# Two transformer blocks in one kernel: layers unrolled with one panel stream, and the banded heads' steps reordered

## The reference

```python
h = _rms_norm(x, in_norm_g[l]); y = h @ w_in[l] + b_in[l]
m_h = mlstm_chunkwise(...)         # 4 heads of 64, stabilised exponential gates
h_h = hgrn2_chunkwise(...)         # 4 heads of 64, decay per channel
s_out = swa_sink_attention(...)    # 8 query, 2 key heads of 64, window 128, RMS norm and rotation of q and k
x = x + concat([m_out, h_out, s_out]) @ w_out[l]
x = x + square(relu(_rms_norm(x) @ w_up[l])) @ w_down[l]
x = x + sigmoid(_rms_norm(x) @ w_ple_gate[l]) * _rms_norm(p[l] @ w_ple_proj[l])
```

## Time and profile before

| what | value |
|---|---|
| median of 3 runs | 3120.99 us (3120.82 to 3121.11) |
| profiled execution | 3119.96 us |
| its span, first to last instruction | 3118.2 us |
| PE busy | 2886.8 us, 93% of the span |
| DVE, ACT, POOL busy | 1637.1, 1113.8, 162.9 us |
| mean granted clock of PE | 0.947 |
| DMA | 281.06 MB, 90 GB/s |

### The profile page before, as it was taken

One profiled execution on the slowest core, in us unless ns is written; L12 is line 12 of the kernel. 1 busy time (PEld: TensorE's weight loads), 2 busy tenths in 40 slices (PEclk: granted clock), 3 DMA queues, 4 the chain that ended last, 5 costly groups with the idle time before them and its releaser, 6 DMA issues. The chain is left out here.

```text
span 3118.2 us, 37948 instructions
## 1 busy us (share of the span) xinstructions
PE 2886.8 (93%) x14756; PEld 2357.1 (76%) x14756; DVE 1637.1 (53%) x2921; ACT 1113.8 (36%) x1712; POOL 162.9 (5%) x160
## 2 busy tenths in 40 slices
PE   6988899999798899999987998899997998899998
PEld 5777788887686777888866877788886787778886
DVE  5736566655664557555665544553544543464442
ACT  6434322224353433222344344332322444332231
POOL 1200000002121000000020000000000000000000
PEclk9987899999898889999988999999998999999999
DMA  4110144443221013444403111222322210122322
GB/s 151 68 41 28 41 176 175 150 152 111 90 84 41 28 41 132 154 160 162 162 34 128 62 35 35 68 86 97 108 73 92 68 53 19 65 89 76 113 78 78
DMA packets 43282, 281.06 MB, mean 90 GB/s; under 512 B 6105, under 2 KB 6361, under 8 KB 11737
## 3 DMA queue, kind: packets, MB, share of 16 engines
q1 hardware_dynamic: 43096, 278.54, 25.7%
HBM read 276.42 MB, written 2.10 MB: 89 GB/s over the span
## 5 line engine op out<-in xcount | busy, mean ns | idle before, releaser
L304 DVE TENSOR_TENSOR low_panels<-raw_panels,high_panels 128x2048 fp32r<-128x2048 f32 (+3 forms) x218 | 469.3, 2153 | 325.9 <-ACT high_panels L292 325.8
L292 ACT ACTIVATE high_panels<-raw_panels 128x2048 fp32r<-128x2048 f32 (+3 forms) x218 | 392.5, 1801 | 475.3 <-PE bank L1492 152.0
L421 PE MATMUL bank<-mlp_h_high,high_panels 128*128 128x512 f32 x1152 | 457.1, 397 | 0.0
L421 PE MATMUL bank<-mlp_h_low,high_panels 128*128 128x512 f32 x1152 | 455.2, 395 | 0.0
L421 PE MATMUL bank<-mlp_h_high,low_panels 128*128 128x512 f32 x1152 | 455.0, 395 | 0.0
L421 PEld LDWEIGHTS bank<-mlp_h_high,low_panels 128*128 128x128 f32 x1152 | 215.9, 187 | 52.8
L421 PEld LDWEIGHTS bank<-mlp_h_high,high_panels 128*128 128x128 f32 x1152 | 216.0, 188 | 52.0
L421 PEld LDWEIGHTS bank<-mlp_h_low,high_panels 128*128 128x128 f32 x1152 | 216.0, 188 | 51.6
L446 PE MATMUL bank<-high_panels,h_high 128*128 128x256 f32 x704 | 213.1, 303 | 8.4 <-DVE arena L1179 7.8
L421 PE MATMUL bank<-h_high,high_panels 128*128 128x512 f32 x496 | 207.2, 418 | 0.2
L1492 PE MATMUL bank<-mlp_hid_high,high_panels 128*128 128x512 f32 x512 | 204.3, 399 | 0.0
(11 more groups left out here) (349 smaller groups left out, 5068.5 us busy)
## 6 DMA issues: line engine op xcount, KB each, us to landing
raw_panels<-in_w SPq DMA_DIRECT2D x238, 1024.0 KB, 4.9
raw_panels<-in_w SPq DMA_DIRECT2D x16, 384.0 KB, 3.2
raw_panels<-in_w SPq DMA_DIRECT2D x4, 960.0 KB, 4.7
raw_panels<-in_w SPq DMA_DIRECT2D x4, 768.0 KB, 4.3
row<-in_row SPq DMA_DIRECT2D x2, 1220.0 KB
x<-in_xT SPq DMA_DIRECT2D x2, 1024.0 KB, 6.1
raw_panels<-in_w SPq DMA_DIRECT2D x4, 512.0 KB, 3.5
mix<-in_rope SPq DMA_DIRECT2D x2, 1024.0 KB, 8.3
```

Source lines behind the costliest of these rows:

```text
L292: self.nc.scalar.activation(self.g.high[:, i % SPLIT, 0:raw.shape[1]], raw, ACT.Copy).then_inc(self.high_ready, 1)
L304: self.nc.vector.tensor_tensor(self.g.low[:, i % SPLIT, 0:w], raw, self.g.high[:, i % SPLIT, 0:w].bitcast(F32), ALU.subtract).then_inc(sel ...
L421: ins = nc.tensor.matmul(bank[:, :], w[a][:, k, c0:c0 + P], rhs[b][:, k0 + k, :], start=first and k == 0 and j == 0, stop=last and k == kt ...
```

## The change

The loops are gone: layers are Python loops, and every stage of every layer stands in the program. A `Stream` holds the panels of all four layers in order, and a `Panels` view of one layer counts from its offsets, so that the two panels ahead may belong to the next layer. Each stage makes its own semaphores; Pool clears those of the stage before. The gains, biases and vectors of all layers are loaded once at the start, the mask `causal` goes to the second part's table, which is loaded in `layer_two`, and 1 + scale times gain is made in `embedding_gate`.

```diff
+class Stages:
+    def begin(self):
+        self.old = self.now
+        stack = ExitStack()
+        self.now = (Semaphores(self.nc, stack, self.n), stack)
+        self.n += 1
+        return self.now[0], [] if self.old is None else list(self.old[0].made.values())
+def clear(pool, used):
+    for sem in used:
+        pool.sem_clear(sem)
-def clear_semaphores(nc, s):
...
+class Stream:
+    def __init__(self, nc, g, s, layers):
+        ...
+        for dram, l, panels in layers:
+            for panel, (at, w) in zip(panels, offsets(panels)[0]):
+                if panel[0] != "w_mod_2":
+                    self.split.append(len(self.all))
+                self.all.append((dram[l, :, at:at + w], w))
...
 # Panels (a view of one layer; n0, i0 are its offsets in the stream)
+    def loads(self, sp, first, last):
+        lo = RAW + (0 if self.i0 == 0 and first == AHEAD else self.stream.upto(self.i0 + first))
+        for n in range(lo, min(self.stream.upto(self.i0 + last) + RAW, len(self.stream.all))):
             sp.wait_ge(self.low_ready, n - RAW + 1)
+            self.stream.load(sp, n)
     def high(self, act, i, products=None, value=0):
+        j = self.i0 + i
+        if j >= len(self.stream.split):
             return
...
 # part_one, start block
-                pan.load_first(sp, 0, s("first_panel_loaded"))
+                for n in range(RAW):
+                    views[0].stream.load(sp, n)
+                # (biases, vec2 and the final gain of all layers, then a wait for them)
+                for i in range(AHEAD):
+                    views[0].low(dve, i)      # ACT: views[0].high(act, i), behind its exponentials
-        with nc.Fori(0, DEPTH) as l:
-            layer_one(...)
+        for l in range(DEPTH):
+            layer_one(nc, g, a, views[l], l, k1, vecs[:, l, :], row, gbs[:, l, :], cs, bounds[:, l, :, :], small)
+            mlp_one(nc, g, views[l], l, vecs[:, l, :])
+            embedding_gate(nc, g, a, views[l], l, vecs[:, l, :], vec2[:, l, :])
...
 # layer_one
+                clear(pool, used)                       # Pool, behind its memset
-                norm_scalar(nc, act, g, e, hh, before={0: lambda: pan.high(act, 0), 3: lambda: pan.high(act, 1)})
+                norm_scalar(nc, act, g, e, hh)
-                norm_vector(..., before={1: lambda: pan.low(dve, 0), 4: lambda: pan.low(dve, 1)})
+                norm_vector(nc, dve, g, e, x, vec[:, V_GIN:V_GIN + DC], hh, hl)
 # DVE, token groups: the low split now follows the eviction
-                    if i == at_panel[n]:
+                    if i == at_panel[n] and kind != "token":
                         pan.low(dve, n + AHEAD)
...
+                        if i == at_panel[n]:
+                            pan.low(dve, n + AHEAD)
 # PE, levels
-                    if k == 15:
+                    if k == 18:
                         turn_gates()
-                    if k == 17:
-                        spread(0)
+                spread(0)                               # behind the last step
 # ACT: conv_open, sigmoid and exponential of step 17 now behind keep_apart(n_levels - 1)
 # DVE: gates(4) of step 16 now behind keep(n_levels - 1)
-            dense_m.setdefault(3 * i // 4, []).append(j)
+            dense_m.setdefault(i // 2, []).append(j)
 # DVE, blocks: the groups' evictions now ahead of block_probs(j)
-                    if 10 <= j < 14:
-                        rotate(j - 10)
+                    if j == 8:
+                        invert_window()                 # reciprocal of ss, then w_rstd; roots on ACT at j == 7, was 9
+                pool.wait_ge(s("w_rstd"), 1)            # Pool, behind the spans
+                for t in range(NT):
+                    rotate(t)                           # the same operations, on nc.gpsimd
 # banded heads
-        masked = region(7168, 1536, "p (i t) -> p i t", i=3)
+        masked = region(7168, 1536, "p (i t) -> p i t", i=6)
+        def score_bank(p, m):
+            return bank[3 + 2 * (p % 2) + m]
+        def chunk_bank(c):
+            return bank[1 + (chunk_after[c] + 1) % 2]
-                    if p >= 1:
-                        pe.wait_ge(w.max_ready, 2 * p)
+                    if p >= 2:
+                        pe.wait_ge(w.max_ready, 2 * (p - 1))
-                        nc.scalar.activation(turned[:, m, 0:n], bank[5 + m][:, 0:n], ACT.Copy)...   # twice
+                    nc.scalar.activation(turned[:, :, 0:n], bank[7]...[:, :, 0:n], ACT.Copy).then_inc(w.turned_kept, 1)
+                    behind = [chunk_at[c] for c in chunk_after if chunk_after[c] == i - 1]
+                    if behind:
+                        pe.wait_ge(chunk_low, max(behind) + 1)     # a group waits for the chunk in its bank
 # PE, step p (ACT: softmax(p), keep_turned(p - 2), then silu, groups, chunks; DVE: softmax(p), normalise(p - 3), ...)
-                    if 2 <= p < n_pairs + 2:
-                        result(p - 2)
-                    if 1 <= p < n_pairs + 1:
-                        turn(p - 1)
-                    chunks, then dense groups
+                    if 3 <= p < n_pairs + 3:
+                        result(p - 3)
+                    if 2 <= p < n_pairs + 2:
+                        turn(p - 2)
+                    dense groups, then chunks
...
 # embedding_gate (ACT high and DVE low alike), and mlp_two through its last calls
-                    if c == 2:
-                        pan.high(act, first + 4, full, DC + 2)
+                    if c in (2, 4, 6):
+                        pan.high(act, first + 3 + c // 2, full, DC + c)
-                pan.load_next_layers(sp, l)
```

More of the change, by code:

```diff
@@ L252, in __init__ @@
             self.first.setdefault(panels[n][0], i)
-        self.nsplit = len(self.split)
-    def loads(self, sp, l, first, last):
-        lo = RAW if first == 0 else self.upto(first) + RAW
-        for n in range(lo, min(self.upto(last) + RAW, self.n)):
-            sp.wait_ge(self.low_ready, n - RAW + 1)
-            self.load(sp, l, n)
     def upto(self, i):
         return 0 if i <= 0 else self.split[min(i, self.nsplit) - 1] + 1
-    def load(self, sp, l, n):
-        a, w = self.off[n]
-        sp.dma_start(self.g.raw[:, n % RAW, 0:w], self.dram[l, :, a:a + w]).then_inc(self.loaded[n % RAW], 16)
@@ L297, in low @@
+        if j >= len(self.stream.split):
             return
-        for n in range(self.upto(i), self.split[i]):
-            between(dve, n)
-        n = self.split[i]
-        w = self.off[n][1]
-        dve.wait_ge(self.high_ready, i + 1)
+        n = self.stream.split[j]
+        for m in range(self.stream.upto(j), n):
+            between(dve, m - self.n0)
+        w = self.stream.all[n][1]
+        dve.wait_ge(self.high_ready, j + 1)
         raw = self.g.raw[:, n % RAW, 0:w]
-        self.nc.vector.tensor_tensor(self.g.low[:, i % SPLIT, 0:w], raw, self.g.high[:, i % SPLIT, 0:w].bitcast(F32),
+        self.nc.vector.tensor_tensor(self.g.low[:, j % SPLIT, 0:w], raw, self.g.high[:, j % SPLIT, 0:w].bitcast(F32),
@@ L305, in low @@
                                      ALU.subtract).then_inc(self.low_ready, 1)
     def parts(self, pe, i):
-        n = self.split[i]
+        j = self.i0 + i
+        n = self.stream.split[j]
         pe.wait_ge(self.low_ready, n + 1)
-        kt, w = self.panels[n][2], self.off[n][1]
-        return [t[:, i % SPLIT, 0:w].rearrange("p (k c) -> p k c", k=kt) for t in (self.g.high, self.g.low)]
+        kt, w = self.panels[self.split[i]][2], self.stream.all[n][1]
+        return [t[:, j % SPLIT, 0:w].rearrange("p (k c) -> p k c", k=kt) for t in (self.g.high, self.g.low)]
@@ L1576, in _, with embedding_gate @@
                 nc.vector.tensor_tensor(g.mod_all[:, l, :], g.bank[7][:, 0:6 * DC], vec[:, V_BMOD:V_BMOD + 6 * DC], ALU.add)
-def embedding_gate(nc, g, a, s, pan, l, vec):
+    g.stages.end()
+def embedding_gate(nc, g, a, pan, l, vec, vec2):
+    s, used = g.stages.begin()
     x = g.x
@@ L2205, in _, with mlp_two @@
                     dense(i)
-    mlp_two(nc, g, s, pan, l, vec, mod)
-    clear_semaphores(nc, s)
-def mlp_two(nc, g, s, pan, l, vec, mod):
+    g.stages.end()
+def mlp_two(nc, g, pan, l, vec, mod):
+    s, used = g.stages.begin()
     x = g.x
```

400 lines of the change are left out of this document (193 added, 207 removed).

## The result

The changed kernel takes 3009.43 us (median of 4 runs, 3004.78 to 3011.59) against 3120.9 us for the kernel before (3117.34 to 3121.11). The ratio is 0.9644, with a 95% interval of 0.9632 to 0.9655. The profiled execution took 3004.78 us.

What follows compares the result with a forecast made beforehand. PE's own work, its holes and its slow-clock stretches were taken as the bound, with only holes and slow stretches winnable; terms summed to -77.4 us on a 3118.2 us span, giving 3043.5 us, range 3012 to 3080.

Steps and rivals of the forecast that it cites:

- three boundaries: Layer boundaries: clearing, barrier, jump back and per-layer loads go, leaving 6.49 us each; -36.9 us.
- end of the program: Program end: one clearing and loop exit go, idle before the last spreading falls from 3.97 to 2.09 us; -1.9 us.
- start, to the first product: Program start: the first two panels' splits now precede the norm with nothing hiding them; +2.6 us, bounds 0 and 5.
- levels, to the first block's scores, two layers: Gated heads' levels: two queue-order waits go and the clock recovers; -10.5 us a layer, bounds -14 and -6.
- blocks and rotation, to the first pair's scores: Block stage: window projections packed into 6 blocks, rotation moved to Pool; -3.3 us a layer, bounds -10 and +18.
- banded heads, to the end of the layer: Banded heads: second score banks, single copy and longer lag cut idle and slow clock; -8 us a layer, bounds -21 and +2.
- splits at the tails, and the rest: Three stage tails: splitting the next layer's panels delays DVE's last x updates, 0.8 us a place; +2.4 us.
- the clock holds: Rival, chance 0.14: PE stays at the upper clock level through levels and banded heads; 3013 us.
- code-loading rival: Rival, chance 0.03: each of 12 unrolled stage starts pays for its first instructions; at 8 us each, 3140 us.
- the eviction ahead of the split: Levels: evicting a token group before the low split was to help by 2 us.
- Pool's rotation: Block stage: Pool instead of DVE rotates the banded heads, taking 23 us a layer, with PE waiting for it.
- the rival that rested on this: Rival, chance 0.09: Pool's reads are locked out, the rotation takes 43.5 + 3 instead of 23 us; 3090 us.

Runs made afterwards that it cites:

- after_h32: The changed kernel with 8 unused columns (32 bytes) ahead of the stage tensors, no instruction changed: 3047.37 us, 0.9779 of the kernel before.
- rotate_dve: The changed kernel with the window heads' rotation back on DVE, four pieces at blocks 10 to 13: 3005.9 us, 0.9631 of the kernel before.
- lag_two: The changed kernel with the banded heads' old lag (transposes one pair behind, results two), new banks and buffers kept: 3005.14 us, 0.9632 of the kernel before.
- buffers_old: The changed kernel with the banded heads' old lag, one pair of score banks, three score buffers and one eviction per head: 3027.16 us, 0.9701 of the kernel before.

## Why the prediction missed

At equal pitch the forecast can be read term by term. The run after_h32 has the pitch of the kernel before (233.3 ns in all four feed-forward stages) and otherwise the whole change; its span is 3043.3 us, where the forecast's span was 3040.8.

| term | predicted, us | before to after_h32, us |
|---|---|---|
| three boundaries | -36.9 | -36.6 (2.08 + 4.39, 2.08 + 4.55 twice, as in the changed kernel) |
| end of the program | -1.9 | -1.9 (the same) |
| start, to the first product | +2.6 | +3.4 |
| levels, to the first block's scores, two layers | -21.0 | -19.9 |
| blocks and rotation, to the first pair's scores | -6.6 | -14.3 |
| banded heads, to the end of the layer | -16.0 | -7.4 |
| splits at the tails, and the rest | +2.4 | +1.8 (the remainder) |
| sum, on the span | -77.4 | -74.9 |
| pitch of the products | 0 | -40.4 (after_h32 to after: 3043.3 to 3002.9; by the medians -37.9) |

**The step that failed** is in the first paragraph: "The change leaves the matmuls as they are, so it can win only holes and slow stretches." It leaves their number and order, not their duration. The diff showed that tables in front of the activations changed their sizes and places; I read it for what it loads and not for where it puts the rest. The forecast of 3043.5 us is the time of the changed kernel with the old pitch (3047.37) within 4 us. None of the rivals was the right one: "the clock holds" gives 3013 us, near the result, but by another mechanism; the clock rose from 0.947 to 0.958 already in the part that was forecast (0.960 in after_h32).

**Boundaries, end, levels.** Right in place, mechanism and size. No stage start shows the hole of the code-loading rival: 2.08 us of idle ahead of the spreading at all three boundaries. In the levels DVE is late next, by up to 2.9 us, as forecast. Inside the levels one term was too small: the eviction ahead of the split was put at 2 us a layer, and undoing it cost 6 (83.6 to 89.9 us). Undoing the order cost 11. Together that is more than the 10 us a layer that the levels gained at equal pitch, so the two overlap.

**Start.** Right in sign, 0.8 us too small.

**Blocks and rotation.** The gain was forecast 8 us too small, and the reason I gave was wrong. Pool's rotation itself came out as forecast: 21.0 us from 208.02 to 229.05 (23 predicted), as these rows of Pool in the first layer show, its first operations and its last:

```profile
208.02 1.26 POOL L740 TENSOR_TENSOR arena<-arena,small 128x640 f32<-128x640 f32 x1 [60.41 <-DVE small L1352]
209.35 1.54 POOL L741 TENSOR_TENSOR arena<-arena,row 128x640 f32<-128x640 f32 x1
210.97 2.15 POOL L747 TENSOR_TENSOR arena<-arena,cos_sin 128x80 f32<-128x80 f32 x4
...
228.70 0.35 POOL L750 TENSOR_TENSOR arena<-arena 128x80 f32<-128x80 f32 x1
```

But it bought nothing: DVE can do it at no cost that was measured. What paid is a line that I had counted only in the levels ("evicting a token group before the low split helps by 2 us there"): over the levels and the blocks it is worth 15 us by the medians.

The rotation did meet one large operation of DVE with both inputs in on-chip memory, the squares of the heads' outputs:

```profile
209.94 2.04 DVE L1357 TENSOR_TENSOR arena<-arena 128x1024 f32<-128x1024 f32 x1
```

It began while Pool's second operation ran and took 2.04 us, where rotate_dve and the kernel before have 1.22 us for it. Pool's next operation, the first of the four at 210.97, began while it ran and took 1.22 us, where the median of its kind is 0.35. In both cases the one that came second was the one drawn out. By the Trainium skill, "SBUF — State Buffer", section "Who interferes with whom", Pool's reads are locked out while DVE holds two SBUF inputs, and the other way round. The trace agrees, at 0.8 us for DVE and 0.9 for Pool in this layer. Pool's operations of 640 elements stayed at 1.26 and 1.54 us, far from the 23.5 us a layer of the rival that rested on this.

**Banded heads.** Half the size that was forecast, and won by the second pair of banks, the six buffers and the single eviction (22 us between lag_two and buffers_old), not by the lag. I had listed all of them and priced none by itself. Undoing them costs more than the whole stage had gained on the kernel before (90.3 us in buffers_old, 86.4 before). Either the rest of the change in this stage (the chunks on the projections' banks, among others) cost something, or buffers_old is worse than the old arrangement because both heads share bank 7; that was not separated.

## What to carry to other kernels

Before costing a change, compare not only the instructions but also where its tensors will lie: a table that changes its size moves everything allocated behind it, and here 32 bytes were worth 34 to 38 us of 3000, as much as the three boundaries together. When a kernel is tuned, try a few pads ahead of the operands of its dense stages, and when two versions are compared, hold the distance between those operands equal. And of a set of edits made together, the cheapest (one eviction ahead of one split, 15 us) can be the one that pays while the most elaborate ones (rotation on Pool, longer lag) pay nothing.

## What the runs showed of the hardware

The pitch of back-to-back products of 128x128 by 512 columns, in stages with a mean granted clock of 0.97 to 0.99, depended on the distance between the stationary and the moving operand in on-chip memory: 226.7 to 229.2 ns at 0, 64, 256, 512 and 832 bytes modulo 1024, 232.3 or 232.4 at 128 and 233.3 or 233.4 at 32, 96 and 800, with one stage at 832 that ran at 233.3 where its twin ran at 228.9. A common shift of both operands by 32 bytes made no difference. Why the distance matters, no run shows. By the Trainium skill, "TensorE: Matmul & The Clock Gate", section "Step-by-step: what each phase is for", the two operands are read through two independent ports; by "SBUF — State Buffer", section "Who interferes with whom", TensorE never waits on anyone. Neither has a place for what these runs show, and here the measurement decides.

The granted clock of a layer differed between kernels with the same instructions. The second run of `layer_one` of the changed kernel, and then that of after_all32, which is the same code with everything shifted (columns as above):

```profile
800.00:1124.20 324.20, 294.13 (x1912) 246.62 (x1912) 183.49 (x411) 148.98 (x294) 55.74 (x74) 0.91 0.16 54
```
```profile
801.00:1130.30 329.30, 299.84 (x1913) 251.59 (x1913) 183.36 (x411) 148.93 (x294) 55.85 (x74) 0.89 0.16 53
```

The same matmuls, 6 us more of busy time at a clock of 0.89 in place of 0.91. An effect of a few microseconds can be hidden or feigned by this, which is why they were read from single stages here.
